# A two-block transformer kernel: its input in four pieces on ScalarE's queue, turned one chunk at a time

## The chip, the cores and the metric

The kernel runs on one core of one Trainium2 chip. The metric is the time of one execution on the device in microseconds, the median of several runs. The engines are PE (TensorE, matmul and transpose), DVE (VectorE), ACT (ScalarE), POOL (GpSimd) and SP (SyncE, which here only issues DMAs). ACT and POOL can issue DMAs too.

## The reference

There are 256 tokens of 1024 columns in float32. The first block is an RMS norm, one projection, two attentions in parallel (one with rotary keys per head, one with low-rank latents), gates, an output projection and an MLP. The second block is a gated mixer with a dilated attention, then a product-key expert layer over 16384 experts. What matters here is only how the first block begins:

```python
h = _rms_norm(x, g_pre_mix[l])          # x * rsqrt(mean(x*x) + eps) * g
proj = h @ w_in[l]                      # 1024 x 4256
qa, ka, va, c_q, c_kv, k_r, gate_logits = _split_cols(proj, ...)
```

The factor of each row, rsqrt(mean(x*x) + eps), is applied to the result of the projection, so that the multiplication can start before it is known. Only the gain g goes into the operand.

## The kernel before

**Data.** X is the input in SBUF, two tiles of 128 tokens by 1024 columns. For the projections it must stand with its columns on the partitions: PE transposes chunk c (128 columns of both tiles, two transposes, line 471) into a PSUM bank, ACT reads the bank, multiplies by the gain and writes the rounded high half TH (line 974), DVE computes the rest TL (line 1405). Every weight unit (128 rows of up to 1024 columns) is treated the same way: a DMA of SP brings it into one of four buffers `raw`, ACT rounds it into `whi` (line 968), DVE computes `wlo` (line 1396). `split(u)` in ACT's and DVE's programs is this step; each has three buffers. A product then is three matmuls: TH x whi, TH x wlo, TL x whi (line 453 where the weights move, `rows`).

**Order.** Every engine has a program written out by hand, and the programs meet by semaphores only. The first projection has eight units IN_A + k of 672 columns (336 KB each); unit k multiplies chunk k of X, 12 matmuls of 336 columns. Then come twelve units of 1024 columns (512 KB each), 12 matmuls of 512 columns. A counter s runs over the steps: one per unit for the first eight, two per unit afterwards. At each step every engine does its part of the main work and then `beside(s)`, which holds the work that goes on beside the projections: for PE, ACT and DVE those are the functions of that name. For the first eight steps ACT and DVE do `split(s + 2)`, then `beside(s)`.

**The start.** SP issues cst (identity and other constants, 148 KB), X columns 0 to 255, posi (the positions, 1 KB), unit 0, X columns 256 to 511, X columns 512 to 1023, and then the other units as their buffers come free. POOL issues ppc (the gains, 34.5 KB), mask_c (256 KB) and gb1 (a vector spread over 128 partitions, 512 KB). PE turns chunks 0 to 3 ahead of unit 0 and chunks 4 to 7 behind it (`beside(0)`). ACT loads its first function table at its first activation.

**The row factor.** ACT squares and sums tile 0 of X (line 977) at s = 2, behind `warm(ACT.Sqrt)`, which loads the table of the square root; DVE does tile 1 at s = 3. At s = 4 the factor r1 is worked out, at s = 5 two diagonal matrices of it, and at s = 7 PE multiplies them with ones (line 547) so that the factor stands along the free axis (rbc). At s = 8 to 10 DVE copies rbc and works out the angles of the rotation from posi. r1 is first needed when the results of the eight units are read (s = 8).

## Time and profile before

| | |
|---|---|
| median of 3 runs | 1370.74 us (1369.51 to 1370.87) |
| the profiled execution | 1368.58 us, its span 1366.8 us |
| PE busy | 1316.4 us, 96% of the span |
| DVE, ACT busy | 943.5 us (69%), 690.4 us (51%) |
| DMA | 260.55 MB, mean 191 GB/s |

The span runs from the first to the last instruction of the profiled execution, and all times in the trace count from its start. Busy time of an engine is the sum of its instructions. In a timeline a row is a run of equal instructions: start, time from the first start to the last end, engine, line, operation, result and operands, count, and in brackets how long the engine was idle before and what released it.

### The profile page before, as it was taken

Reading aid. Unit: us, or ns where it says so; the run is one execution under the profiler, and the core shown is the slowest. Engines: PE = TensorE matmul, PEld = TensorE weight load, DVE = VectorE, ACT = ScalarE, POOL = GpSimd, SP = SyncE. Lnnn points to the kernel's source line nnn. Section 1 sums busy time; section 2 is a strip of 40 time slices with the busy share of each in tenths; the row PEclk is TensorE's granted clock in tenths of the full one; section 3 lists DMA queues with packets and bytes.
Section 4 is the critical chain, followed back from the end, with each engine's and each line's share of the span. In section 5 each row is a group of like instructions: output and inputs, shape, how many; then the busy total and the mean of one; then the engine's idle time right before and its main releaser. Section 6 shows DMA issues by size and latency. Waiting matters only on the chain.

```text
span 1366.8 us, 22018 instructions
## 1 busy us (share of the span) xinstructions
PE 1316.4 (96%) x8592; PEld 1200.9 (88%) x8592; DVE 943.5 (69%) x1792; ACT 690.4 (51%) x1135; POOL 33.1 (2%) x27
## 2 busy tenths in 40 slices
PE   7999998999989899999999999999999999999996
PEld 6889978998877678999999999999988888888885
DVE  5765676674456755999899666676667676767665
ACT  5566456664455744444454444444444545454553
POOL 0000130000020000000000000000000000000000
PEclk9999999999999998999999999999999999999999
DMA  7533455666646335477767655555567676766763
GB/s 241 165 122 111 141 171 155 184 184 187 194 147 195 126 102 174 145 237 228 228 218 237 190 169 170 185 171 157 169 225 264 234 245 234 248 249 239 244 235 106
DMA packets 72662, 260.55 MB, mean 191 GB/s; under 512 B 8224, under 2 KB 8864, under 8 KB 72304
## 3 DMA queue, kind: packets, MB, share of 16 engines
q1 hardware_dynamic: 71520, 255.77, 57.7%
q0 software_dynamic: 1040, 3.38, 0.8%
q8 instruction: 69, 1.13, 0.3%
q14 instruction: 33, 0.27, 0.1%
HBM read 240.25 MB, written 18.87 MB: 190 GB/s over the span
## 4 chain that ended last, share of the span: by engine, by line
PE 87%; DVE 5%; ACT 4%; DMA 2%; issue 1%; SPq 0%; DVEq 0%; ACTq 0%
PE ps L933 24%; PE ps L453 14%; PE ps L461 13%; PE ps L462 13%; PE ps L463 13%; PE ps L916 4%; ACT whi L968 1%; PE ps L496 1%; DVE wlo L1396 1%; DVE mg L1654 1%; DMA raw<-in_expert_v_dram 1%; PE ps L471 1%; DMA raw<-in_w_in_dram 1%; PE ps L477 1%; DMA X<-in_x_dram 1%
## 5 line engine op out<-in xcount | busy, mean ns | idle before, releaser
L1396 DVE TENSOR_TENSOR wlo<-raw,whi 128x1024 fp32r<-128x1024 f32 (+2 forms) x410 | 498.0, 1216 | 352.8 <-ACT whi L968 350.7
L968 ACT ACTIVATE whi<-raw 128x1024 fp32r<-128x1024 f32 (+2 forms) x421 | 441.5, 1050 | 443.6 <-PE ps L463 166.0
L461 PE MATMUL ps<-TH,whi 128*128 128x256 f32 x1536 | 443.3, 289 | 2.3 <-DVE TL L1405 1.2
L462 PE MATMUL ps<-TL,whi 128*128 128x256 f32 x1536 | 436.3, 284 | 0.0
L463 PE MATMUL ps<-TH,wlo 128*128 128x256 f32 x1536 | 435.8, 284 | 0.0
L461 PEld LDWEIGHTS ps<-TH,whi 128*128 128x128 f32 x1536 | 296.9, 193 | 3.2 <-issue 3.0
L462 PEld LDWEIGHTS ps<-TL,whi 128*128 128x128 f32 x1536 | 296.3, 193 | 0.0
L463 PEld LDWEIGHTS ps<-TH,wlo 128*128 128x128 f32 x1536 | 295.7, 193 | 0.0
L933 PE MATMUL ps<-whi,TH 128*128 128x512 f32 x512 | 199.5, 390 | 5.2 <-DVE wlo L1396 3.7
L933 PE MATMUL ps<-whi,TL 128*128 128x512 f32 x512 | 199.2, 389 | 0.0
L933 PE MATMUL ps<-wlo,TH 128*128 128x512 f32 x512 | 199.2, 389 | 0.0
L933 PEld LDWEIGHTS ps<-whi,TH 128*128 128x128 f32 x512 | 96.1, 188 | 26.1 <-DVE wlo L1396 4.5
L933 PEld LDWEIGHTS ps<-whi,TL 128*128 128x128 f32 x512 | 96.1, 188 | 20.1
L933 PEld LDWEIGHTS ps<-wlo,TH 128*128 128x128 f32 x512 | 96.1, 188 | 19.7
L1334 ACT ACTIVATE ACTV<-ps 128x512 f32<-128x512 f32 x64 | 38.3, 598 | 123.9 <-PE ps L916 123.9
L453 PE MATMUL ps<-whi,TH 128*128 128x512 f32 (+1 forms) x208 | 79.1, 393 | 6.5 <-DVE wlo L1396 2.7
L453 PE MATMUL ps<-wlo,TH 128*128 128x512 f32 (+1 forms) x208 | 77.1, 383 | 0.0
L453 PE MATMUL ps<-whi,TL 128*128 128x512 f32 (+1 forms) x208 | 77.0, 383 | 0.0
L916 PE MATMUL ps<-X 128*128 128x128 f16 x512 | 70.7, 296 | 0.1
L2013 DVE TENSOR_TENSOR TL<-ACTV,TH 128x256 fp32r<-128x256 f32 x128 | 55.6, 434 | 0.5 <-ACT TH L974 0.5
L916 PEld LDWEIGHTS ps<-X 128*128 128x128 f16 x512 | 52.2, 118 | 3.6 <-DVE X L1999 0.3
L2009 DVE TENSOR_TENSOR ACTV<-ACTV,stage 128x256 f32<-128x256 f32 x128 | 53.6, 420 | 1.7 <-ACT ACTV L1334 1.7
(292 smaller groups left out, 1365.3 us busy)
## 6 DMA issues: line engine op xcount, KB each, us to landing
raw<-in_expert_u_dram SPq DMA_DIRECT2D x128, 512.0 KB, 3.7
raw<-in_expert_v_dram SPq DMA_DIRECT2D x128, 512.0 KB, 3.6
raw<-in_w_up_dram SPq DMA_DIRECT2D x32, 512.0 KB, 3.7
raw<-in_w_down_dram SPq DMA_DIRECT2D x32, 512.0 KB, 4.3
acts<-stage SPq DMA_DIRECT2D x32, 512.0 KB, 4.1
stage<-acts SPq DMA_DIRECT2D x30, 512.0 KB, 3.3
raw<-in_w_in_dram SPq DMA_DIRECT2D x20, 512.0 KB, 4.3
raw<-in_w_gate_dram SPq DMA_DIRECT2D x16, 512.0 KB, 3.5
```

Of the source, the lines that this page charges most:

```text
L453: m = e.matmul(o, x[:, k0 + j, sl], w[:, h, c:c + step], start=first, stop=last)
L461: e.matmul(dst, whi[:, h, sl], xh[:, k, :], start=k == 0, stop=False)
L462: e.matmul(dst, whi[:, h, sl], xl[:, k, :], start=False, stop=False)
L463: m = e.matmul(dst, wlo[:, h, sl], xh[:, k, :], start=False, stop=k == kn - 1)
L471: m = e.transpose(ps[b][:, at + t * 128:at + t * 128 + 128], src[:, t, c * 128:c * 128 + 128], ident)
L916: m = e.matmul(ps[g % 4][:, i * 128:i * 128 + 128], room[:, g % 2, 0, :, i], room[:, g % 2, w, :, i], start=w == 1, stop=w == 2)
L933: m = e.matmul(ps[bank4(t, d)][:, :], x[:, n % 8, sl], w[:, h, d * 512:d * 512 + 512], start=n == 0 and k == 0, stop=n == 127 and k == 2)
L968: e.activation(whi[:, u % NH, 0:n], raw[:, u % NR, 0:n], ACT.Copy).then_inc(*hi(u))
L1334: e.activation(ACTV[:, :, 4 * g:4 * g + 4], ps[g % 4][:, :].rearrange("p (t k) -> p k t", t=4), ACT.Copy, scale=1.0 / G_SCALE).then_inc(*w ...
L1396: e.tensor_tensor(wlo[:, u % NH, 0:n], raw[:, u % NR, 0:n], whi[:, u % NH, 0:n].bitcast(F32), ALU.subtract).then_inc(*lo(u))
L2009: e.tensor_tensor(ACTV[:, v, :], ACTV[:, v, :], stage[:, v % 8, :], ALU.mult).then_inc(*taken_v(i))
L2013: e.tensor_tensor(TL[:, i % 8, :], ACTV[:, V_ORDER[i], :], TH[:, i % 8, :].bitcast(F32), ALU.subtract).then_inc(*cut_d(i))
```

## The change

X comes in four pieces of 1, 1, 2 and 4 chunks, issued by ACT at its very start. SP issues only the identity ahead of the weight units, and the rest of cst behind unit 3. posi moves from SP to POOL, and POOL issues posi, mask_c and gb1 only when TL of chunk 5 is written. DVE writes a tile of zeros, and PE multiplies it four times (128 rows, 512 columns, into bank 7, whose content nothing reads) before it waits for the identity. ACT's first function table is loaded by `warm(ACT.Copy)` right behind its DMA issues. PE turns chunks 0 and 1 ahead of unit 0 and chunk s + 2 behind unit s; the banks are 4 to 7 in turn. In steps 0 to 5 ACT and DVE do `beside(s)`, now with chunk s + 2, ahead of `split(s + 2)`. The squares move to s = 5, r1 to s = 6, the diagonals to s = 7, rbc and the angles to s = 9.

```diff
--- before.py
+++ after.py
@@ -140,6 +140,9 @@
 
         ident = cs("ident")
         x_rows = A["x"].rearrange("(t p) d -> p t d", p=128)
+
+        X_PIECES = [(0, 1), (1, 2), (2, 4), (4, 8)]
+        PIECE_OF = [0, 1, 2, 2, 3, 3, 3, 3]
         warm_in, warm_out = stat(1), stat(1)
 
 
@@ -166,6 +169,7 @@
         PT1 = sb(p1, "PT", [128, 2, 8, 128])
         o1 = sb(p1, "o1", [128, 2, 512])
         gb1 = sb(p1, "gb1", [128, 1024])
+        zeros = sb(p1, "zeros", [128, 512], F32R)
         posi = sb(p1, "posi", [128, 2], I32)
         posf = sb(p1, "posf", [128, 2])
         ang = sb(p1, "ang", [128, 2, 24])
@@ -303,8 +307,8 @@
 
 
 
-        d_cst, d_ppc, d_pos, d_gb1, d_mask_c = (landing(n) for n in ("cst", "ppc", "pos", "gb1", "mask_c"))
-        d_x = [landing(f"x{i}") for i in range(3)]
+        d_ident, d_cst, d_ppc, d_pos, d_gb1, d_mask_c = (landing(n) for n in ("ident", "cst", "ppc", "pos", "gb1", "mask_c"))
+        d_x = [landing(f"x{i}") for i in range(4)]
         d_raw = [landing(f"raw{i}", range(i, UNITS, NR)) for i in range(NR)]
         d_gb2, d_gb4, d_cos, d_sin, d_mask_d, d_lng, d_lnb, d_ws, d_sub = (
             landing(n) for n in ("gb2", "gb4", "cos2", "sin2", "mask_d", "lng", "lnb", "ws", "sub"))
@@ -399,9 +403,9 @@
         out_d = signal("out_d", (
             "moba0r moba0 moba1r moba1 mla0r mla0 mla1r mla1 dil0r dil0 dil1r dil1").split())
         norm_d = signal("norm_d", (
-            "ones ss1 v1 r1 diag0 diag1 rbc pos ang0 ang1 turns whole less0 less1 less2 held folded angles "
-            "cq.ss cq.v cq.r cq ck.ss ck.v ck.r ck out.v out.r rsq down.v down.r ab.v ab.r x4.v x4.r x4.0 "
-            "x4.1").split())
+            "ones zeros ss1 v1 r1 diag0 diag1 rbc pos ang0 ang1 turns whole less0 less1 less2 held folded "
+            "angles cq.ss cq.v cq.r cq ck.ss ck.v ck.r ck out.v out.r rsq down.v down.r ab.v ab.r x4.v x4.r "
+            "x4.0 x4.1").split())
         rows_d = signal("rows_d", (
             "lat1 lat3 q k v uq0 uq1 uq2 ukv0 ukv1 q2 k2 v2.0 v2.1").split())
         gate_d = signal("gate_d", range(16))
@@ -499,11 +503,19 @@
 
 
 
-            e.wait_ge(*d_cst.at(0))
-            for c in range(4):
-                if c % 2 == 0:
-                    e.wait_ge(*d_x[c // 2].at(0))
-                turn(X, c, 4 + c).then_inc(*turned(f"x{c}"))
+            e.wait_ge(*norm_d.at("zeros"))
+            for _ in range(4):
+                e.matmul(ps[7][:, :], zeros[:, 0:128], zeros[:, :], start=True, stop=True)
+
+            def turn_x(c):
+                e.wait_ge(*d_x[PIECE_OF[c]].at(0))
+                if c >= 4:
+                    e.wait_ge(*low.at(f"x{c - 4}"))
+                turn(X, c, 4 + c % 4).then_inc(*turned(f"x{c}"))
+
+            e.wait_ge(*d_ident.at(0))
+            turn_x(0)
+            turn_x(1)
 
             def causal_attention(a, n):
 
@@ -537,12 +549,9 @@
 
             def beside(s):
 
-                if s == 0:
-                    e.wait_ge(*d_x[2].at(0))
-                    for c in range(4, 8):
-                        e.wait_ge(*low.at(f"x{c - 4}"))
-                        turn(X, c, c).then_inc(*turned(f"x{c}"))
-                elif s == 7:
+                if s < 6:
+                    turn_x(s + 2)
+                elif s == 9:
                     e.wait_ge(*norm_d.at("diag1"))
                     e.matmul(ps[7][:, 0:256], mg[:, 0, 0, 0:128], mg[:, 1, 0, :], start=True, stop=True).then_inc(*turned("rbc"))
                 elif s == 15:
@@ -998,13 +1007,21 @@
 
 
 
+            for i, (c0, c1) in enumerate(X_PIECES):
+                e.dma_start(X[:, :, c0 * 128:c1 * 128], x_rows[:, :, c0 * 128:c1 * 128]).then_inc(*d_x[i](0))
+            e.wait_ge(*norm_d.at("ones"))
+            warm(ACT.Copy)
+            gain_x = lambda c: pp("g_pre_mix", c)
+
+            def high_x(c):
+                e.wait_ge(*turned.at(f"x{c}"))
+                high_of("x", c, 4 + c % 4, 0, gain_x, TH)
+
             e.wait_ge(*d_ppc.at(0))
-            gain_x = lambda c: pp("g_pre_mix", c)
-            for c in range(4):
-                e.wait_ge(*turned.at(f"x{c}"))
-                high_of("x", c, 4 + c, 0, gain_x, TH)
-                if c % 2:
-                    split(c // 2)
+            high_x(0)
+            split(0)
+            high_x(1)
+            split(1)
 
             def causal_attention(a, n):
                 if n == 3:
@@ -1022,17 +1039,14 @@
                     probs(a, 1, 1, 5)
 
             def beside(s):
-                if s in (0, 1):
-                    for c in (4 + 2 * s, 5 + 2 * s):
-                        e.wait_ge(*turned.at(f"x{c}"))
-                        high_of("x", c, c, 0, gain_x, TH)
-                elif s == 2:
-                    e.wait_ge(*norm_d.at("ones"))
+                if s < 6:
+                    high_x(s + 2)
+                if s == 5:
                     warm(ACT.Sqrt)
-                    for i in range(3):
+                    for i in range(4):
                         e.wait_ge(*d_x[i].at(0))
                     square(SB1[:, 0:4, :].rearrange("p a b -> p (a b)"), X[:, 0, :], ss1[:, 0:1]).then_inc(*norm_a("ss1"))
-                elif s == 4:
+                elif s == 6:
                     e.wait_ge(*norm_d.at("v1"))
                     e.activation(s1, v1, ACT.Sqrt).then_inc(*norm_a("s1"))
                 elif s in (11, 19):
@@ -1120,6 +1134,10 @@
                     e.activation(sg[:, m, :], mg[:, m % 2, 0, :], ACT.Tanh, bias=hb[:, m:m + 1], scale=0.5).then_inc(*gate_a(m))
 
             for s in range(82):
+                if s < 6:
+                    beside(s)
+                    split(s + 2)
+                    continue
                 if s < 8:
                     split(s + 2)
                 elif s % 2 == 0:
@@ -1455,12 +1473,17 @@
 
 
             e.memset(warm_in, 1.0).then_inc(*norm_d("ones"))
+            e.memset(zeros[:, :].bitcast(F32), 0.0).then_inc(*norm_d("zeros"))
+            gain_x = lambda c: pp("g_pre_mix", c)
+
+            def low_x(c):
+                low_of("x", c, 4 + c % 4, 0, gain_x, TH, TL)
+
             e.wait_ge(*d_ppc.at(0))
-            gain_x = lambda c: pp("g_pre_mix", c)
-            for c in range(4):
-                low_of("x", c, 4 + c, 0, gain_x, TH, TL)
-                if c % 2:
-                    split(c // 2)
+            low_x(0)
+            split(0)
+            low_x(1)
+            split(1)
             e.tensor_scalar(hb[:, :], ppc[:, PPC["b_gate"][0]:PPC["b_gate"][1]], 0.5, None, ALU.mult)
 
             def causal_attention(a, n):
@@ -1479,26 +1502,25 @@
                     outs(a, 1, 6)
 
             def beside(s):
-                if s in (0, 1):
-                    for c in (4 + 2 * s, 5 + 2 * s):
-                        low_of("x", c, c, 0, gain_x, TH, TL)
-                elif s == 3:
-                    for i in range(3):
+                if s < 6:
+                    low_x(s + 2)
+                if s == 5:
+                    for i in range(4):
                         e.wait_ge(*d_x[i].at(0))
                     square_sum(SB1[:, 4:8, :].rearrange("p a b -> p (a b)"), X[:, 1, :], ss1[:, 1:2]).then_inc(*norm_d("ss1"))
-                elif s == 4:
+                elif s == 6:
                     e.wait_ge(*norm_a.at("ss1"))
                     e.wait_ge(*norm_d.at("ss1"))
                     mean_eps(v1, ss1, 1024).then_inc(*norm_d("v1"))
                     e.wait_ge(*norm_a.at("s1"))
                     e.reciprocal(r1, s1).then_inc(*norm_d("r1"))
-                elif s == 5:
+                elif s == 7:
                     e.memset(mg[:, 0, 0, 0:128], 1.0)
                     e.wait_ge(*norm_d.at("r1"))
                     e.wait_ge(*d_cst.at(0))
                     for t in range(2):
                         scaled_copy(mg[:, 1, 0, t * 128:t * 128 + 128], ident, r1[:, t:t + 1]).then_inc(*norm_d(f"diag{t}"))
-                elif s == 8:
+                elif s == 9:
                     e.wait_ge(*turned.at("rbc"))
                     e.tensor_copy(rbc[:, :], ps[7][:, 0:256]).then_inc(*norm_d("rbc"))
                     e.wait_ge(*d_pos.at(0))
@@ -1510,7 +1532,6 @@
                     e.tensor_scalar(an2[:, :, :], ang[:, :, :], INV2PI, MAGIC, ALU.mult, ALU.add).then_inc(*norm_d("turns"))
                     e.wait_ge(*norm_d.at("turns"))
                     e.tensor_scalar(an3[:, :, :], an2[:, :, :], MAGIC, None, ALU.subtract).then_inc(*norm_d("whole"))
-                elif s == 9:
                     for i, c in enumerate((PI_A, PI_B, PI_C)):
                         e.wait_ge(*norm_d.at(f"less{i - 1}" if i else "whole"))
                         e.scalar_tensor_tensor(out=ang[:, :, :], in0=an3[:, :, :], scalar=-c, in1=ang[:, :, :],
@@ -1628,6 +1649,10 @@
                                        op0=ALU.add, op1=ALU.mult).then_inc(*scaled_d(n))
 
             for s in range(82):
+                if s < 6:
+                    beside(s)
+                    split(s + 2)
+                    continue
                 if s < 8:
                     split(s + 2)
                 elif s % 2 == 0:
@@ -2078,6 +2103,8 @@
                                 ALU.subtract).then_inc(*lo_pool(u))
 
             e.dma_start(ppc[:, :], A["ppc"]).then_inc(*d_ppc(0))
+            e.wait_ge(*low.at("x5"))
+            e.dma_start(posi[:, :], A["positions"]).then_inc(*d_pos(0))
             e.dma_start(mask_c[:, :, :], A["causal"]).then_inc(*d_mask_c(0))
             e.dma_start(gb1[:, :], A["g_post_mix"].partition_broadcast(128)).then_inc(*d_gb1(0))
             for u in (BR_B + 1, BR_B + 2, BR_B + 3, OUT, OUT + 1, UP, UP + 1):
@@ -2114,9 +2141,6 @@
                         e.wait_ge(*lo.at(u - NR))
                 e.dma_start(raw[:, u % NR, 0:width(u)], units[u]).then_inc(*d_raw[u % NR](u))
 
-            def load_x(i, c0, c1):
-                e.dma_start(X[:, :, c0:c1], x_rows[:, :, c0:c1]).then_inc(*d_x[i](0))
-
             def store(j):
                 e.wait_ge(*gelu_u.at(4 * j + 3))
                 e.dma_start(acts[j], stage[:, 4 * (j % 2):4 * (j % 2) + 4, :]).then_inc(*d_store[j % 2](j))
@@ -2128,14 +2152,11 @@
                 e.wait_ge(*taken_v.at(4 * j + 3))
                 e.dma_start(stage[:, 4 * (j % 2):4 * (j % 2) + 4, :], acts[j]).then_inc(*d_fetch[j % 2](j))
 
-            e.dma_start(cst[:, :], A["cst"]).then_inc(*d_cst(0))
-            load_x(0, 0, 256)
-            e.dma_start(posi[:, :], A["positions"]).then_inc(*d_pos(0))
-            load(0)
-            load_x(1, 256, 512)
-            load_x(2, 512, 1024)
-            for u in range(1, QUERY + 4):
+            e.dma_start(ident, A["cst"][:, 0:128]).then_inc(*d_ident(0))
+            for u in range(QUERY + 4):
                 load(u)
+                if u == 3:
+                    e.dma_start(cst[:, 128:CST_W], A["cst"][:, 128:CST_W]).then_inc(*d_cst(0))
             e.wait_ge(*norm_a.at("x4.1"))
             e.wait_ge(*norm_d.at("x4.1"))
             e.wait_ge(*last_d.at("11"))
```

## Rows read from the trace of the kernel before

**Rows 1.** The page: the chain of work that ended last, by line.
```profile
PE ps L933 24%; PE ps L453 14%; PE ps L461 13%; PE ps L462 13%; PE ps L463 13%; PE ps L916 4%; ACT whi L968 1%; PE ps L496 1%; DVE wlo L1396 1%; DVE mg L1654 1%; DMA raw<-in_expert_v_dram 1%; PE ps L471 1%; DMA raw<-in_w_in_dram 1%; PE ps L477 1%; DMA X<-in_x_dram 1%
```

**Rows 2.** Windows of the start: length, busy us of each engine, PEclk, DMA share, GB/s.
```profile
8.00:10.00 2.00, 0.00 (x0) 0.00 (x0) 0.86 (x1) 0.76 (x1) 0.00 (x0) 1.00 1.03 366
...
20.00:24.00 4.00, 4.00 (x28) 4.00 (x27) 2.27 (x4) 2.35 (x4) 0.00 (x0) 1.00 0.63 151
```

**Rows 3.** Timeline of the start, 0 to 24 us.
```profile
1.26 0.68 POOL L2080 DMA_DIRECT2D ppc<-in_ppc_dram  x1 [0.81 <-POOLq L2262]
1.66 0.46 SPq L2133 DMA_DIRECT2D posi<-in_positions_dram  x1
...
4.04 1.09 PE L471 MATMUL ps<-cst,X 128*128 128x128 f32 x4 [4.04 <-DMA X<-in_x_dram]
4.79 1.28 ACT L974 ACT_TABLE_LOAD   x1 [4.79 <-PE ps L471]
6.08 0.84 ACT L974 ACTIVATE TH<-ps,ppc 128x256 fp32r<-128x256 f32 x2
...
8.23 0.76 ACT L968 ACTIVATE whi<-raw 128x672 fp32r<-128x672 f32 x1 [1.31 <-DMA raw<-in_w_in_a_dram]
9.02 0.86 DVE L1396 TENSOR_TENSOR wlo<-raw,whi 128x672 fp32r<-128x672 f32 x1 [1.48 <-ACT whi L968]
...
10.05 1.12 PE L471 MATMUL ps<-cst,X 128*128 128x128 f32 x4 [4.92 <-DMA X<-in_x_dram]
...
10.82 0.91 PE L453 MATMUL ps<-whi,TH 128*128 128x336 f32 x2
...
14.32 1.45 PE L471 MATMUL ps<-cst,X 128*128 128x128 f32 x8
...
15.53 0.56 PE L453 MATMUL ps<-whi,TH 128*128 128x336 f32 x2
...
18.50 1.28 ACT L971 ACT_TABLE_LOAD   x1
...
20.95 1.41 ACT L968 ACTIVATE whi<-raw 128x672 fp32r<-128x672 f32 x2
```

**Rows 4.** Waits of PE over the whole span: total us, times, longest.
```profile
PE ps L471 <- DMA X<-in_x_dram: 9.0, 2, 4.9
PE ps L471 <- DVE X L1686: 6.4, 2, 3.4
...
PE ps L471 <- ACT xn L974: 3.2, 1, 3.2
```

**Rows 5.** Timeline of PE, 24 to 48 us.
```profile
28.50 0.59 PE L547 MATMUL ps<-mg 128*128 128x256 f32 x2
28.74 0.58 PE L453 MATMUL ps<-whi,TH 128*128 128x512 f32 x1
...
39.84 0.60 PE L471 MATMUL ps<-cst,pj 128*128 128x128 f32 x4
40.20 0.48 PE L453 MATMUL ps<-whi,TH 128*128 128x512 f32 x1
...
43.53 0.44 PE L471 MATMUL ps<-cst,pj 128*128 128x128 f32 x2 [0.34 <-DVE CQl L1405]
```

**Rows 6.** Windows behind three pauses of PE: length, PE busy, PEclk, DMA.
```profile
209.80:216.50 6.70, 5.36 (x24) 0.50 0.23 76
...
400.90:404.20 3.30, 3.30 (x13) 0.50 0.02 5
...
513.60:523.70 10.10, 7.87 (x36) 0.50 0.68 208
```

**Rows 7.** DMA issues of the first 2.2 us: count, KB, us to landing.
```profile
raw<-in_w_in_a_dram SPq DMA_DIRECT2D x1, 336.0 KB, 6.0
X<-in_x_dram SPq DMA_DIRECT2D x1, 256.0 KB, 2.7
...
ppc<-in_ppc_dram POOLq DMA_DIRECT2D x1, 34.5 KB, 2.8
```

## The prediction

> **What bounds the kernel now.** I read the page's chain first: almost all of it is PE's dense work, and of the start there is only "PE ps L471" and "DMA X", 1% each [rows 1]. A change at the start can be worth no more than what it takes out of the first microseconds, and it keeps that only if PE, once it runs, is not made to wait again. So I read the start by stretches [rows 2], then the timeline to 24 us [rows 3], then who waits for whom [rows 4], the timeline to 44 us, where the old and the new order of work meet again [rows 5], and what PE's clock did after earlier pauses [rows 6].
>
> From 8 to 10 us PE has nothing while the DMA engines are over 100% busy [rows 2]. The waiter is L471, the transposes of X: twice, at most 4.9 us [rows 4]. From 10.05 on PE works without a gap. The first projection starts at 10.82, the last of the eight input units ends at 28.50, the two matmuls of L547 follow, and the next twelve units start at 28.74 [rows 3, 5]. PE is slow at first: rows 0 take 3.50 us (10.82 to 14.32), while the seven units from 15.53 to 28.50 take 1.85 each. So the engine ran at 1.2 GHz and then at 2.4 (the profile's own clock reads 1.00 throughout and is no help here). When did it rise? The eight transposes at 14.32 take 1.21 us to the next row; at the low level they would take 1.54 (four in 0.77, 10.05 to 10.82), at the high one 0.72 (four in 0.36, 39.84 to 40.20 in [rows 5]). So it rose at about 15.2, 5.1 us after PE began to work unbroken.
>
> **Part 1, the start.** ACT now issues four DMAs before anything else. SP's issues take about 0.46, POOL's first 0.68 [rows 3]. ACT's queue is a plain one like SP's, so I take 0.46: 0.75 to 2.6 us. The table load, 1.28, moves there too, from 4.79, where it was on the path; with 0.2 for the warm-up ACT is free at 4.1 (at POOL's price 5.0). The first x piece is half of the 256 KB that landed 2.7 us after their issue [rows 7]; issued at 0.75 it lands at 3.0 to 3.5 and is turned 0.75 later (4.04 to 4.79). ppc is issued as before, at 1.26, and lands 2.8 later, at 4.1. So the first high part runs 4.15 to 4.6. The first weight unit leaves SP right behind the identity, at 1.2. Before, it left at 2.16, behind posi, and took 6.0 us [rows 7], beside mask_c and the broadcast of gb1, which are both held back now. Bounds for its landing: 2.7 us, as X's piece, gives 3.9; 6.0 gives 7.2. Beside it now stands up to 1 MB of x on its own queue, in place of 0.77 MB of constants; but it starts 1 us earlier into emptier engines. I take 3.5 us, 4.7. Then whi 0.76, wlo 0.86 and hand-overs: the first projection starts at **6.4** against 10.82, **4.4 us earlier** (6.1 to 8.9 by the bounds).
>
> The Trainium skill, "DMA: Bandwidth & Descriptors", section "Issuing engines are not separate DMA queues", says that DMAs of several issuers run on the same 16 engines and interleave, so that a second issuer saves only issue time. The full engines of [rows 2] agree. By that rule alone part 1 would gain from what is held back and from SP's issue time, nothing else.
>
> POOL now waits for low x5 (about 18 us) ahead of posi, mask_c and gb1; behind them on POOL stand only its own splits, the first that of unit 46. posi is first read by DVE after rows 7, mask_c and gb1 far later. The 0.77 MB takes 2.1 us at the 366 GB/s of [rows 2], at a time when the engines are 63% busy and a weight unit has over 4 us between issue and split. The rest of cst lands long before the diagonals behind step 7. All this: nothing. The memset of 512 columns of zeros takes less than the 0.86 of a 672-column DVE pass, and DVE has nothing to do until 4.6. Four matmuls of 512 columns at the low clock take 4 x 0.44 by the 3.50/12 of a 336-column one: 1.8 us, over by 3.5, in PE's wait for x. Nothing as long as x lands no earlier; at most 0.5.
>
> **Part 2, chunk by chunk.** PE turns chunk k+2 behind rows k, ACT then does high x(k+2) and splits unit k+2, DVE the low halves. From the end of rows k: two transposes 0.44 ([rows 5], at 43.53), high 0.42, whi 0.76, wlo 0.86, hand-overs 0.09. Rows k+2 may start **2.57** after the end of rows k. PE has rows k+1 (1.84 at 2.4 GHz) and one or two turns of 0.18 until then, so about every second unit waits 0.37. With the clock up 5.1 us after 6.4, at 11.5: rows 0 run 6.4 to 9.9, a turn 0.39, rows 1 to 12.71 (1.2 us at the low level, 34% of it, the rest fast), rows 2 12.89 to 14.73, rows 3 15.28 to 17.12, rows 4 17.30 to 19.14, rows 5 19.69 to 21.53, rows 6 21.71 to 23.55.
>
> **Part 3, the square.** At step 5 ACT does high x7, then warm(Sqrt), the square of X, and only then split(7). Before, the same block stood behind split(4) and delayed only split(5): 18.50 to 20.95, with wlo 5 ready at 22.6 (20.95 + 0.76 + 0.86) for rows 5 at 22.9, just hidden. Now what queues behind it is the very unit that PE wants next but one. From the end of rows 5: transposes 0.44, high 0.47, table load, warm and square 2.45, whi 0.76, wlo 0.86, hand-overs 0.09. Rows 7 start **5.07** later, at 26.60. PE has only rows 6, until 23.55: it **stands 3.05 us**. DVE's own square lies inside ACT's block. Rows 7 end at 28.44, against 28.50: **-0.06**. In terms: -4.42 start; +0.74 two waits of 0.37; +3.05; +0.57 rows 1 still partly slow; +0.08 turns; the rest is rounding.
>
> **Part 4, behind it.** The rbc matmul moves from behind unit 7 to behind unit 8, 0.24 either way. wlo 8 is done about 6.5 after the end of rows 5, and rows 8 start at 6.91. On DVE the reciprocal, the diagonals, the rbc copy, the angles and the cq norm come later relative to PE. Bounds 0 and 0.5; PE idled 0.34 at 43.53 for CQl anyway, which takes up a small delay. I take nothing.
>
> **Part 5, the clock.** A standing PE has a second price. Three times PE stood that long: 6.4 us in two pauses of which the longer was 3.4, and one of 3.2 [rows 4]; each time the granted clock was then 0.50, that is 1.2 GHz, for stretches of 6.7, 3.3 and 10.1 us [rows 6]. Part 3 makes a fourth such pause. The shortest stretch costs half its length, **1.7**, since dense rows 7 and 8 follow. Bounds: 0 (no fall; here the pause lies between dense rows, there short transposes with further pauses followed) and 5. I take 1.7, by three falls out of three.
>
> Sum: -0.06 + 1.7 = +1.6. The profiled execution took 1368.58 (its span 1366.8 and 1.8 around it), 2.2 below the median of 1370.74; on it the sum makes 1370.2. On the median, which I forecast, it makes **1372.4**.
>
> **The rivals.**
> *No fall.* The pause comes, the clock stays: -0.06, 1370.7. For it: dense matmuls on both sides.
> *The zeros lift the clock early.* PE then has matmuls or turns from 1.7 to about 5 us. If it runs at 2.4 GHz from 6.4 on, the chain of 2.57 sets the pace: rows 0 end at 8.24, rows 1 run 8.5 to 10.34, rows 2 10.81 to 12.65, rows 3 end at 14.75, rows 4 at 17.06, rows 5 at 19.16, rows 7 at 26.07: -2.4, 1368.3, or 1370.0 with a fall. Against it: PE stands from 5 to 6.4, and the 1.09 us of transposes at 4.04 lifted nothing. The Trainium skill, "TensorE: Matmul & The Clock Gate", Part 1, says that the low level is the default and that activity lifts it, and Part 4 that transposes do not count as such; the rise after the dense stretch from 10.05 goes with the first. By it this rival hangs on the zeros alone.
> *The slow side: x beside the weights.* x's four pieces take a share of every DMA engine, so the first weight unit again lands 6.0 us after its issue, at 7.2. Rows 0 start at 8.9, +2.5: 1374.9 with the fall, 1373.2 without. For it: the engines are full before PE starts. Against it: fewer bytes ahead. With the fall it decides (over +0.2%) from a landing at 5.8.
> *Much faster.* The clock is up early, does not fall, and the pause is shorter than 3.05 or the start earlier than 6.4: under 1368.
>
> **How the numbers follow.** A measurement of this kernel can tell about 0.2% (2.7 us) from no change. Forecast 0.38, no fall 0.26, early clock 0.16, x beside the weights 0.13, much faster 0.07. The range 1368.1 to 1374.2 holds the first three with most of their bounds and leaves out most of the last two. Faster (below 1368.0): 0.07 and 0.04 of the early clock. Slower (above 1373.5): 0.09 of x beside the weights and 0.07 of the forecast with a longer low stretch. So 0.11, 0.73, 0.16.
>
> **What the new profile would show.** The table load before 4; x0 turned near 4.1; the first L453 near 6.4; two idles of PE of some 0.4; then one of 3 us near 24, released by DVE wlo behind ACT whi behind the square; PEclk 0.50 right after it; rows 7 ending within 1 us of 28.5. I am wrong if the first weight unit lands after 5.8, if the clock is up before 8, or if the pause is under 2 us.

## The result, and the profile after

The changed kernel took **1371.34 us** (median of 20 runs, 1366.99 to 1375.79). The kernel before, run beside it on the same chips, took 1368.15 (20 runs, 1363.71 to 1370.87). The ratio is **1.0027**, with an interval of 1.0015 to 1.0039: some 3.7 us slower (the two medians stand 3.2 apart). The forecast was 1372.4, that is 1.7 above the median shown with it, 1370.74; the direction and the mechanism held, and the size was about half. That the 1372.4 itself lies within 1.1 us of the measured median is in part luck: the kernel before came out 2.6 us lower this time. The profiled execution has a span of 1369.8 us against 1366.8.

**The start** (timeline of the changed kernel; it answers to [rows 3]; L475 is the transpose, L457 the projection, L983 the high half, L977 and L1414 the two halves of a weight unit):

```profile
0.74 2.03 ACTq L1011 DMA_DIRECT2D X<-in_x_dram  x4
...
1.25 0.68 POOL L2105 DMA_DIRECT2D ppc<-in_ppc_dram  x1 [0.80 <-POOLq L2283]
...
1.49 2.07 PE L508 MATMUL ps<-zeros 128*128 128x512 f32 x4 [1.49 <-DVE zeros L1476]
2.79 1.28 ACT L980 ACT_TABLE_LOAD   x1 [2.79 <-issue]
...
3.90 0.66 PE L475 MATMUL ps<-cst,X 128*128 128x128 f32 x2 [0.34 <-DMA X<-in_x_dram]
...
5.03 0.69 PE L475 MATMUL ps<-cst,X 128*128 128x128 f32 x2 [0.47 <-DMA X<-in_x_dram]
6.11 0.47 ACT L983 ACTIVATE TH<-ps,ppc 128x256 fp32r<-128x256 f32 x1 [1.82 <-DMA ppc<-in_ppc_dram]
6.48 0.75 ACT L977 ACTIVATE whi<-raw 128x672 fp32r<-128x672 f32 x1
...
8.18 0.93 PE L457 MATMUL ps<-whi,TH 128*128 128x336 f32 x2 [2.46 <-DVE wlo L1414]
...
13.81 0.72 PE L457 MATMUL ps<-whi,TH 128*128 128x336 f32 x2
...
14.37 0.47 PE L457 MATMUL ps<-wlo,TH 128*128 128x336 f32 x2
```

The issues, the table load and x0 come as forecast. Then ACT stands for 1.82 us, and what it waits for is ppc, the smallest transfer of the start. The DMA issues of the first 3 us (count, KB, us from issue to landing; beside [rows 7]):

```profile
raw<-in_w_in_a_dram SPq DMA_DIRECT2D x4, 336.0 KB, 6.2
X<-in_x_dram ACTq DMA_DIRECT2D x1, 512.0 KB, 8.7
X<-in_x_dram ACTq DMA_DIRECT2D x2, 128.0 KB, 3.4
...
ppc<-in_ppc_dram POOLq DMA_DIRECT2D x1, 34.5 KB, 4.8
```

ppc took 4.8 us here and 2.8 before. The first projection starts at 8.18, which is 2.6 us earlier than before [rows 3] and not 4.4. The step in the durations, 0.72 to 0.47, shows that PE's clock rose at about 14.4.

**The pause** (same timeline). The two short waits for the chain, which stand at the weight loads of rows 3 and rows 5, and the long one:

```profile
17.48 0.30 PEld L457 LDWEIGHTS ps<-whi,TH 128*128 128x128 f32 x2 [0.29 <-DVE wlo L1414]
...
21.93 0.30 PEld L457 LDWEIGHTS ps<-whi,TH 128*128 128x128 f32 x2 [0.29 <-DVE wlo L1414]
...
24.79 1.28 ACT L980 ACT_TABLE_LOAD   x1
...
26.19 1.04 ACT L986 ACTIVATE SB<-X 128x1024 f32<-128x1024 f32 x1
...
27.23 1.69 ACT L977 ACTIVATE whi<-raw 128x672 fp32r<-128x672 f32 x2
28.01 2.17 DVE L1414 TENSOR_TENSOR wlo<-raw,whi 128x672 fp32r<-128x672 f32 x2 [1.58 <-ACT whi L977]
...
28.92 0.93 PE L457 MATMUL ps<-whi,TH 128*128 128x336 f32 x2 [2.82 <-DVE wlo L1414]
```

In this order it reads as one chain: table load, square, whi 7, wlo 7, and PE's rows 7 at 28.92, after 2.82 us in which PE has nothing. In the windows around it (length, PE busy, PEclk, DMA share, GB/s) the granted clock falls within the pause and is back at 34.9. The 0.85 of the second window is 0.8 us at the low clock, so that the low stretch runs from 28.0 to 34.85, 6.8 us:

```profile
23.00:26.00 3.00, 3.00 (x21) 1.00 0.92 314
26.20:28.80 2.60, 0.00 (x0) 0.85 0.79 303
28.90:34.80 5.90, 5.88 (x18) 0.50 0.72 215
34.90:38.00 3.10, 3.10 (x15) 1.00 0.71 234
```

From 28.92 to 34.85 PE is 100% busy at 1.2 GHz. That is 5.93 us for 2.97 us of work at 2.4 GHz.

**The meeting point.** From the first cq transposes on, both kernels do the same in the same order. They stood at 39.84 [rows 5]:

```profile
44.97 0.60 PE L475 MATMUL ps<-cst,pj 128*128 128x128 f32 x4
48.66 0.44 PE L475 MATMUL ps<-cst,pj 128*128 128x128 f32 x2 [0.34 <-DVE CQl L1423]
```

So the changed kernel is 5.1 us late there. It keeps this offset until about 200 us, where the stretches of low clock begin that the kernel before has too [rows 6]. Those of the changed kernel, in windows as above:

```profile
215.80:222.50 6.70, 5.57 (x26) 0.50 0.24 81
403.50:410.20 6.70, 5.69 (x22) 0.50 0.17 69
519.50:522.90 3.40, 2.82 (x14) 0.51 0.48 193
```

Together they are 16.8 us against 20.1 in [rows 6]. The offset at the end is 3.0 us, not 5.1; half the difference of the stretches is 1.7 of these 2.1. Between the stretches the starts of PE's instructions run parallel in the two traces, but for two steps of 0.5 us, near 424 and 1020 us.

### The profile page after: what moved, and what is told of

It is laid out like the page before. It is cut to its first block, busy times and chain, and to the rows that moved or that the text cites. A ratio compares the mean times of both kernels' runs of the same rounds, so it can differ in the third digit from the quotient of the medians.

```text
span 1369.8 us, 22035 instructions
## 1 busy us (share of the span) xinstructions
PE 1322.0 (97%) x8596; PEld 1203.8 (88%) x8596; DVE 944.5 (69%) x1793; ACT 690.5 (50%) x1136; POOL 33.6 (2%) x28
## 3 DMA queue, kind: packets, MB, share of 16 engines
q10 hardware_dynamic: 1088, 1.05, 0.2%
## 4 chain that ended last, share of the span: by engine, by line
PE 86%; DVE 6%; ACT 5%; DMA 2%; issue 2%; DVEq 0%; SPq 0%; ACTq 0%; POOLq 0%
PE ps L942 24%; PE ps L457 14%; PE ps L465 13%; PE ps L466 13%; PE ps L467 13%; PE ps L925 4%; ACT whi L977 1%; DVE wlo L1414 1%; PE ps L500 1%; DVE mg L1679 1%; PE ps L481 1%; PE ps L878 1%; DMA raw<-in_w_in_dram 1%; PE ps L493 0%; DMA raw<-in_expert_v_dram 0%
## 5 line engine op out<-in xcount | busy, mean ns | idle before, releaser
L1414 DVE TENSOR_TENSOR wlo<-raw,whi 128x1024 fp32r<-128x1024 f32 (+2 forms) x410 | 497.9, 1216 | 348.6 <-ACT whi L977 346.3
L977 ACT ACTIVATE whi<-raw 128x1024 fp32r<-128x1024 f32 (+2 forms) x421 | 441.7, 1051 | 440.4 <-PE ps L467 164.7
L942 PEld LDWEIGHTS ps<-whi,TH 128*128 128x128 f32 x512 | 96.1, 188 | 25.7 <-DVE wlo L1414 3.9
L457 PE MATMUL ps<-whi,TH 128*128 128x512 f32 (+1 forms) x208 | 81.5, 405 | 11.3 <-DVE wlo L1414 7.5
L457 PE MATMUL ps<-wlo,TH 128*128 128x512 f32 (+1 forms) x208 | 78.5, 391 | 0.0
L457 PE MATMUL ps<-whi,TL 128*128 128x512 f32 (+1 forms) x208 | 78.2, 390 | 0.0
L457 PEld LDWEIGHTS ps<-whi,TH 128*128 128x128 f32 x208 | 40.4, 199 | 21.2 <-DVE wlo L1414 9.6
```

The lines of the kernel that those rows point to most:

```text
L457: m = e.matmul(o, x[:, k0 + j, sl], w[:, h, c:c + step], start=first, stop=last)
L942: m = e.matmul(ps[bank4(t, d)][:, :], x[:, n % 8, sl], w[:, h, d * 512:d * 512 + 512], start=n == 0 and k == 0, stop=n == 127 and k == 2)
L977: e.activation(whi[:, u % NH, 0:n], raw[:, u % NR, 0:n], ACT.Copy).then_inc(*hi(u))
L1414: e.tensor_tensor(wlo[:, u % NH, 0:n], raw[:, u % NR, 0:n], whi[:, u % NH, 0:n].bitcast(F32), ALU.subtract).then_inc(*lo(u))
```

## The experiments

Each is one edit to the changed kernel, except the last two, which edit the kernel before. In the table, "start" is the first projection, "pause" PE's idle time at rows 7, "low" what the granted clock spent at 1.2 GHz right behind it, "cq" the meeting point in the profiled execution, and the ratio is the timed one against the kernel before, with its interval. All but the ratio come from one execution each.

| | start | pause | low | cq | ratio |
|---|---|---|---|---|---|
| before | 10.82 | none | none | 39.84 | 1 |
| after | 8.18 | 2.82 | 6.8 | 44.97 | 1.0027 (1.0015 to 1.0039) |
| square_late | 8.69 | 0.28 | none | 40.64 | 1.0007 (0.9993 to 1.0022) |
| fill_pause | 7.28 | filled | none | 39.96 | 1.0010 (0.9995 to 1.0026) |
| sqrt_first | 7.68 | 1.31 | none | 39.87 | 1.0008 (0.9995 to 1.0021) |
| ppc_sp | 8.88 | 2.81 | none | 42.78 | 1.0035 (1.0017 to 1.0053) |
| no_zeros | 7.90 | 2.83 | 6.8 | 44.64 | 1.0026 (1.0010 to 1.0042) |
| bridge | 8.11 | 2.52 | 3.4 | 41.15 | 1.0037 (1.0024 to 1.0050) |
| staged | 7.13 | 2.82 | 3.4 | 42.53 | 1.0014 (0.9998 to 1.0031) |
| early_const | 8.14 | 2.52 | 3.4 | 42.79 | 1.0023 (1.0007 to 1.0038) |
| all_moved | 7.32 | 0.27 | none | 39.07 | 1.0013 (0.9999 to 1.0027) |
| all_moved_bridge | 7.28 | 0.20 | none | 38.52 | 0.9996 (0.9984 to 1.0009) |
| before_zeros | 11.20 | none | none | 39.12 | 0.9989 (0.9973 to 1.0006) |
| before_fill | 10.75 | none | none | 38.81 | 0.9986 (0.9968 to 1.0003) |

Single executions differ where no edit makes them differ. In the seven in which x, unit 0 and ppc are issued as in the changed kernel (after, square_late, fill_pause, sqrt_first, no_zeros, early_const, bridge), ppc took 3.9 to 5.3 us and the start fell between 7.28 and 8.69. In the eight with just the four matmuls by zero (after, square_late, fill_pause, sqrt_first, ppc_sp, staged, early_const, all_moved) the clock rose 3.1 to 6.2 us after the start. A difference between two executions that is smaller than this shows little by itself.

### The square behind the weights: square_late

```diff
-                if s == 5:                    # ACT; DVE's square_sum alike
+                elif s == 7:
                     warm(ACT.Sqrt)
...
                     square(SB1[:, 0:4, :].rearrange("p a b -> p (a b)"), X[:, 0, :], ss1[:, 0:1])
```

The factor r1 and the diagonals follow in the same step, behind the split of unit 9.

> The changed kernel with one thing moved: ACT's square block (warm Sqrt, square, root) and DVE's part of it go from steps 5 and 6 to step 7, behind split(9), with the diagonals behind them. Theory A, the pause behind the square and the fall of the clock after it are the loss: no idle of PE above 0.6 us between rows 0 and rows 11, no granted clock of 0.50 before 60 us; the first L-transpose of cq, at 44.97 in the changed kernel, comes at 39.0 to 39.7 (2.8 of pause and 3.0 of low clock gone), and the kernel is about 5 us faster than the changed one, 0.9985 of before. Rival B, the loss is in the later rbc, angles and norm or in the held-back transfers: those are untouched or later still, cq stays above 43 and the time within 1 us of the changed kernel, 1.002 to 1.003 of before.

The pause is gone, and so is the low stretch:

```profile
26.86 0.58 PE L457 MATMUL ps<-whi,TH 128*128 128x336 f32 x2 [0.28 <-DVE wlo L1413]
40.64 0.66 PE L475 MATMUL ps<-cst,pj 128*128 128x128 f32 x4
45.04 0.44 PE L475 MATMUL ps<-cst,pj 128*128 128x128 f32 x2 [1.00 <-DVE CQl L1422]
```

Although this execution started 0.5 us later than the changed kernel's, it is 4.3 us earlier at the meeting point. So in the trace the place of the square makes the loss. The cq norm now comes later: the wait for CQl grew from 0.34 to 1.00, so that behind it the offset to the kernel before is 1.5 us, not 0.8 (45.04 against 43.53 in [rows 5]). The meeting point is above what was expected in part because the start was 0.5 later, and the time is that of the kernel before, no better; 0.9985 was expected. The timed interval overlaps that of the changed kernel. But the three edits that take away the pause, half of it or the fall behind it (this one and the next two) have ratios of 1.0007 to 1.0010, and the kernels that keep the pause 1.0014 to 1.0037.

### The pause filled: fill_pause

```diff
+                elif s == 6:                  # PE, behind rows 6
+                    for _ in range(12):
+                        e.matmul(ps[4][:, :], zeros[:, 0:128], zeros[:, :], start=True, stop=True)
```

> The changed kernel with 12 more matmuls of zeros (128x512, into a free bank) behind rows 6, so that PE works through the pause: 12 x 0.23 = 2.7 us of work in a wait of 2.8. It prices the clock alone. Theory A, the fall is a price of its own on top of the pause: no 0.50 stretch, rows 7 start within 0.2 us of the changed kernel's time after the end of rows 6, and cq comes 2.5 to 3.4 us earlier than 44.97, at 41.6 to 42.5; 1.0005 of before. Rival C, the low stretch only covers time that would be waited anyway (ACT and DVE set the pace there): cq moves under 1 us, ratio as the changed kernel's, 1.003.

ACT and DVE are as late as in the changed kernel; only PE does not stand idle meanwhile:

```profile
23.93 2.93 PE L556 MATMUL ps<-zeros 128*128 128x512 f32 x12
```

No low stretch followed. From start to meeting point are 32.7 us, against 36.8 in the changed kernel. Of these 4.1 us 1.3 are there when rows 7 start (19.4 us after the start against 20.7; the clock rose 3.1 us behind the start, not 6.2), and 2.8 come behind that, where the low stretch is missing. This separates the two prices of one pause: the standing itself stays (rows 7 start 5.15 us after the end of rows 5, against 5.04), the clock is the other. That no fall came could be chance in one execution, as ppc_sp below shows. The timed ratio is 0.17% below the changed kernel's, but the two intervals overlap.

### The table loaded once: sqrt_first

```diff
-            warm(ACT.Copy)
+            warm(ACT.Sqrt)                    # at ACT's start; none at step 5
```

> The changed kernel with ACT's first warm-up on Sqrt in place of Copy, and the warm-up of Sqrt at step 5 left out: one table load fewer, and the block between high x7 and split(7) shorter by 1.4 us (1.28 load and 0.11). Theory A: the pause of 2.8 us shrinks to 1.4; whether the clock still falls is open, cq at 43.6 if it does, 40.6 if not. If the first rounding after the square root's table needs a load of its own, it shows at 4 us as a second load of 1.28 and the start moves little, since ACT waits for ppc until 6.1. Rival B: cq within 0.5 us of 44.97.

Only one table load is in the trace, at 2.78, and the copies and the square ran behind it. The pause shrank by 1.51, the 1.28 of the load and the 0.2 of the warm-up, and behind a pause of 1.31 us the clock did not fall:

```profile
26.53 0.57 PE L457 MATMUL ps<-whi,TH 128*128 128x336 f32 x2 [1.31 <-DVE wlo L1413]
```

### ppc ahead of the weights: ppc_sp

```diff
             e.dma_start(ident, A["cst"][:, 0:128]).then_inc(*d_ident(0))
+            e.dma_start(ppc[:, :], A["ppc"]).then_inc(*d_ppc(0))      # SP; taken away from POOL
```

> The changed kernel with ppc (the gains) issued by SP right behind the identity, not by POOL. In the changed kernel ACT stood from 4.29 to 6.11 for ppc, which took 4.8 us to land. Theory D, ppc is what made the start 1.8 us later than forecast: ppc lands by 4.2, the first projection starts at 6.6 to 6.9 in place of 8.18, everything to the pause comes 1.3 to 1.6 earlier, the pause stays 2.8; 1 to 1.5 us faster than the changed kernel. Rival E, the weights' landing sets the start anyway: the first unit, now 0.5 later out of SP, lands at 5.2 or later and the projection starts at 7.2 to 8.2, gain under 1 us.

ppc landed at 3.6 and no longer held ACT. The row of unit 0, issued at 1.66 now, and that of ppc:

```profile
raw<-in_w_in_a_dram SPq DMA_DIRECT2D x1, 336.0 KB, 5.5
...
ppc<-in_ppc_dram SPq DMA_DIRECT2D x1, 34.5 KB, 2.4
```

Unit 0 took 5.5 us, where that of the changed kernel, issued at 1.19, took 3.4. ACT stood 2.37 us for it, and the start came at 8.88, later than with ppc late. In the seven executions with ppc on POOL unit 0 took 3.1 to 3.5 us, so its 5.5 lie outside their scatter. Getting one transfer out of the way put another in its place. Why 34.5 KB ahead of it cost unit 0 some 2 us was not found. The Trainium skill, "DMA: Bandwidth & Descriptors", section "Issuing engines are not separate DMA queues", says that DMAs of all issuers interleave on the same 16 engines; that the engines are 91 to 99% busy in the changed kernel from 2 to 8 us agrees with it.

The second finding is what did not happen. Behind a pause of 2.81 us the clock stayed up:

```profile
26.60:29.30 2.70, 0.02 (x1) 1.00 0.87 323
29.40:35.00 5.60, 5.57 (x28) 1.00 0.73 204
```

### The zeros taken out: no_zeros

```diff
-            e.wait_ge(*norm_d.at("zeros"))
-            for _ in range(4):
-                e.matmul(ps[7][:, :], zeros[:, 0:128], zeros[:, :], start=True, stop=True)
```

> The changed kernel without the four matmuls of zeros (the memset stays). Theory F, they do nothing as they stand, since PE waits from 5.7 to 8.2 us behind them: the clock rises 3 to 6.2 us after the first projection, the range of the five profiles so far, x0 is turned up to 0.5 us earlier because PE is free at 3.1, the start does not move since ACT waits for ppc, and the time is within 1 us of the changed kernel's. Rival: they lift the clock earlier in part of the executions: without them the time is 1 to 2 us longer.

The clock rose at about 14.1, 6.2 us behind the start, as in the changed kernel, and the timed ratio is the changed kernel's. So the four matmuls by zero did nothing that shows. How much they move the rise one execution can't say, since with them it came 3.1 to 6.2 us after the start.

### More zeros: bridge

```diff
             turn_x(1)
+            for _ in range(6):
+                e.matmul(ps[7][:, :], zeros[:, 0:128], zeros[:, :], start=True, stop=True)
```

> The changed kernel with six more matmuls of zeros behind the turn of chunk 1 (6 x 0.43 = 2.6 us at the low clock), so that PE works from 1.5 us to the first projection almost without a gap. Theory F, it is the gap from 5.7 to 8.2 us that keeps the four zero matmuls from lifting the clock: the pair of 128x336 matmuls takes 0.47 in place of 0.76 from 9 us at the latest (14.4 in the changed kernel), rows 0 and 1 then take 1.85 to 2.6 and 1.85, and rows 2 start 1.5 to 2.5 us earlier relative to rows 0. The pause of 2.8 stays and grows no shorter; the time is 1 to 2.5 us below the changed kernel's. Rival G, zeros do not lift the clock (its rise hangs on something else): the rise comes 5 to 6 us after the first projection as before and the time is the changed kernel's within 1 us.

Now the first pairs of projections show the step, 0.9 us after the start:

```profile
8.11 0.93 PE L457 MATMUL ps<-whi,TH 128*128 128x336 f32 x2
8.83 0.54 PE L457 MATMUL ps<-wlo,TH 128*128 128x336 f32 x2
9.21 0.47 PE L457 MATMUL ps<-whi,TL 128*128 128x336 f32 x2
```

The 0.9 us lie outside the 3.1 to 6.2 of the eight executions above, and before_zeros below shows the same. So zeros do lift the clock where little stands between them and the work. The Trainium skill, "TensorE: Matmul & The Clock Gate", Part 1, says that activity lifts it from its low default, and this agrees. At the meeting point this execution is 3.8 us ahead of the changed kernel's, and in time its ratio is the highest of all, beside ppc_sp's. Its stretches of low clock behind 200 us:

```profile
210.40:220.50 10.10, 8.66 (x40) 0.50 0.26 75
401.50:404.90 3.40, 3.35 (x16) 0.50 0.13 52
480.00:483.40 3.40, 3.40 (x10) 0.50 0.62 200
517.60:527.70 10.10, 8.18 (x37) 0.50 0.69 227
1353.80:1357.10 3.30, 3.27 (x8) 0.51 0.49 155
```

They are 30.3 us, against 16.8 in the changed kernel and 20.1 in the kernel before: what the start gained is given back there. (Half of the 10.2 on top of the 1.3 at the meeting point would be 6.4; the span is 4.9 longer than before, since PE is not busy through all of them.) This is no accident of one execution: its ten runs lie close together (1371.69 to 1373.50), and the granted clock averaged over a run is 0.986 to 0.989 in all ten, against 0.986 to 0.994 (median 0.9905) in the twenty of the changed kernel. Why these stretches became longer was not found.

### x behind the first weights: staged

```diff
-            for i, (c0, c1) in enumerate(X_PIECES):          # ACT
+            for i, (c0, c1) in enumerate(X_PIECES[:2]):
...
+            load(0)                                          # SP
+            e.wait_ge(*d_ppc.at(0))
+            for u in range(1, QUERY + 4):                    # x2 behind unit 1, x3 behind unit 2
```

> The changed kernel with the transfers of the start staged: ACT issues only the first two x pieces; SP issues the identity and unit 0, then waits for ppc, and then unit 1, x chunks 2 and 3, unit 2, x chunks 4 to 7, unit 3. Theory H, what stands beside them makes ppc (4.8 us in the changed kernel) and unit 0 (up to 7.15 when ppc went first on SP) land late: now ppc lands by 4.3, unit 0 by 4.7, the first projection starts at 6.3 to 6.9 in place of 7.3 to 8.9 over the five profiles. Unit 1 lands by 8, before rows 1 at about 10. Time 1 to 1.5 us below the changed kernel's, the pause of 2.8 stays. Rival I, POOL's queue is slow by itself: ppc lands at 5.2 or later even with few transfers beside it.

With fewer bytes under way unit 0 took 3.3 us, as with all of x, and ppc still 3.8. ppc landed at 5.0 instead of 6.1, and the start came earlier by just that much, at 7.13; 4.3 and 6.3 to 6.9 were expected. This is the earliest start of all, but fill_pause, with all of x under way, had 7.28 and 3.9 us for ppc. With all_moved and all_moved_bridge (7.32, 7.28) three executions with x staged lie at the early end, which speaks for an effect without showing its size. Unit 3 then landed late (PE stood 0.47 at rows 3), and the pause behind the square is unchanged, as it must be. The low stretch was the shorter one this time:

```profile
28.40:31.70 3.30, 3.30 (x12) 0.50 0.75 214
31.80:36.00 4.20, 4.20 (x20) 1.00 0.79 251
```

### The constants not held back: early_const

```diff
             e.dma_start(ppc[:, :], A["ppc"]).then_inc(*d_ppc(0))
-            e.wait_ge(*low.at("x5"))
             e.dma_start(posi[:, :], A["positions"]).then_inc(*d_pos(0))
```

> The changed kernel with posi, mask_c and gb1 not held back (POOL issues them right behind ppc, as before). Theory H, the constants in the start lengthen it: 0.77 MB more ahead of unit 1 and the later x pieces, unit 0 lands at 5 to 7 in place of 4.6, x chunks 4 to 7 above 12, the first projection 0 to 2 us later than 8.18; the pause stays. Time 0 to 2 us above the changed kernel's. Rival B, that held-back transfers collide with the weights at 21 to 27 us and cost there: the time falls by 1 us or more.

The start is at 8.14 (changed kernel 8.18). The 512 KB piece of x took 11.3 us, not 8.7, but no engine needs it so early. Holding back 0.77 MB brought nothing that shows.

### Everything moved: all_moved and all_moved_bridge

The first is staged, with the square late, the table loaded once, and ppc on SP behind unit 0. The second has three more matmuls by zero behind the turn of chunk 1.

> All that the experiments so far point to, in one kernel: the staged transfers, ppc on SP behind unit 0, the warm-up on Sqrt at the start, the square block in step 7. Theory A: each part brings what it brought alone. ppc lands at 4 to 4.5, unit 0 at 4.6, the first projection starts at 6.5 to 6.9; no idle above 0.6 us up to the transposes of cq, no fall of the clock before 60 us; these come at 37.5 to 38.8 (39.84 before). The time is 1 to 2 us below before: ratio 0.998 to 1.000. Rival J, the gain of the start is given back even so, since turning chunk by chunk ties each split to the unit two ahead (2.57 us after each unit) and the clock rises later relative to the work: cq at 39.5 or later, ratio 1.000 to 1.001.

> The same with three more matmuls of zeros (1.3 us) behind the turn of chunk 1, which ends at about 5.6. Theory F: PE works from 1.5 us on almost without a gap, the clock is up by 9 us as in the run with six such matmuls (there 9.0), rows 0 and 1 are fast for the most part, cq at 36.5 to 38; ratio 0.997 to 0.999. If the last matmuls of zeros hold rows 0 up, it is by under 0.3 us. Rival G, the early rise in that run was the luck of one execution: the clock is up 3 to 6 us after the first projection and cq as in the kernel without them.

Both reach the meeting point ahead of the kernel before, but only by 0.8 and 1.3 us, though they start 3.5 us earlier. The chain of 2.5 us for each two units takes most of the rest, and behind the meeting point the waits for CQl (1.00 and 0.98 instead of 0.34) take another 0.6, so that 0.1 and 0.6 are left (43.47 and 42.92 against 43.53). Neither timed ratio can be told from 1. The early rise that was expected of the three further matmuls (by 9 us) did not come: the clock rose at 11.1, 3.8 us after the start, within the range of the executions without them.

### The kernel before, with zeros: before_zeros and before_fill

```diff
+            e.wait_ge(*norm_d.at("zeros"))
+            multiply_zeros(4)
...
             for c in range(4):
+                if c == 2:
+                    multiply_zeros(12)
                 if c % 2 == 0:
                     e.wait_ge(*d_x[c // 2].at(0))
```

before_fill also puts 12 matmuls of TH by TH, of which nothing is read, ahead of the transposes of two later norms.

> The kernel before with nothing of the change but the zeros, and more of them: the memset, four matmuls before the wait for cst, and twelve more (4 to 5 us) between the transposes of chunk 1 and the wait for chunk 2, where PE stood 4.9 us. Theory F, dense zeros lift the clock and the rise is worth half of the low time behind 10.82: the clock is up by 10.5 us (15.2 before), rows 0 take 1.9 us in place of 3.5 and the transposes behind them 0.8 in place of 1.2; cq comes 1.5 to 2.4 us earlier than 39.84; ratio 0.998 to 0.9995. Rival G: the zeros do not matter, cq within 0.5 us of 39.84 and ratio 1.000; or the twelfth ends after 10.05 and the start is late by up to 0.3.

> The same, and twelve matmuls of whatever stands in TH (128x512, 2.7 us, into bank 4, which nothing reads then) in each of two of the three later pauses of PE, ahead of the transposes of h2 (3.05 us of idle, then 6.8 us of low clock in the profile of before) and of h3 (3.38, then 3.4). Their results are never read. Theory A, every long pause of PE is paid twice: no low stretch at 205 to 220 and 395 to 410, each worth 1.7 to 5.1 us; together with the start 4 to 7 us below before, ratio 0.995 to 0.9975. Rival C: the low stretches cover work that is not PE's, or the clock falls anyway in the transposes that follow: low stretches stay and the ratio is that of the kernel with zeros at the start alone.

In before_zeros the zeros run from 5.14 to 10.44, and rows 0 then take 1.93 us where they took 3.50. Of these 1.6 only 0.7 reached the meeting point, since x had landed later and rows 1 stood 0.61 for wlo. In the profiled execution of before_fill the pause at 204 is filled, and a low stretch came all the same, behind the short transposes that follow:

```profile
204.16 2.88 PE L718 MATMUL ps<-TH 128*128 128x512 f32 x12
207.39 1.07 PE L472 MATMUL ps<-cst,X 128*128 128x128 f32 x8 [0.35 <-DVE X L1703]
209.02 1.61 PE L472 MATMUL ps<-cst,X 128*128 128x128 f32 x8 [0.56 <-DVE TL L1421]
211.81 0.55 PE L462 MATMUL ps<-TH,whi 128*128 128x256 f32 x1 [1.18 <-issue]
```

The window behind it:

```profile
211.90:215.10 3.20, 3.20 (x15) 0.50 0.46 163
```

It lasted 3.4 us, as in before_zeros, where the kernel before had 6.8. Behind the second filled pause none came, where the kernel before has one [rows 6]:

```profile
400.90:404.20 3.30, 3.30 (x17) 1.00 0.04 10
```

But two of 3.4 us, at 423 and 478 us, are new. These two kernels have the lowest medians (1366.51 and 1365.51 against 1368.59 beside them), but both intervals include 1.

The trace hides something here, since it shows one of the slower executions. The mean granted clock of before_fill's twelve runs falls into two groups: 0.990 to 0.992 in five, which took 1366.60 to 1370.37 us (the profiled one among them), and 0.995 to 0.996 in seven, which took 1362.85 to 1365.64. No run of before_zeros is above 0.993, and of the 109 of the kernel before one reaches 0.995. So filling two pauses did take out low stretches in seven runs of twelve, and these came out at 0.996 to 0.998 of the kernel before, about what was expected. Which stretches they were is not known, as no such run was traced.

## Why the prediction was right, and where its sizes were off

**The start** was mis-sized. The step "ppc is issued as before, at 1.26, and lands 2.8 later, at 4.1" took its price from one execution of the old order, in which the DMA engines were 75% busy while ppc was under way, against 86% in the changed kernel: ppc landed 4.8 later, at 6.1. Three executions of the old order now give 2.8, 3.3 and 3.6 us, seven of the new one 3.9 to 5.3. The step that looked uncertain, the landing of unit 0 at 4.7, held. So the start came 1.8 us later than forecast. ppc_sp shows that this is not ppc's place alone: moved ahead, it sends unit 0 back to 7.15. That is the landing which the rival "x beside the weights" gave, but the rival itself did not come in the changed kernel, where unit 0 landed at 4.6; what was late was the one transfer whose price the prediction gave no bound. How much of this the bytes of x make, staged does not settle.

**Chunk by chunk** held: rows k + 2 start 2.49 and 2.50 us after the end of rows k (2.57 forecast), with two waits of 0.29 (0.37). The clock rose 6.2 us after the start, not 5.1, so that rows 1 took 3.0 us and not 2.4.

**The square** held nearly to the hundredth: rows 7 start 5.04 us after the end of rows 5, at 23.88 (5.07 forecast), and PE stands 2.82 (3.05). The difference is PE's side: from the end of rows 5, rows 6 with the turn took PE 2.2 us and not 2.0. square_late and sqrt_first show the cause by taking it away in two ways.

**The clock** was right in kind and mis-sized. "The shortest stretch costs half its length, 1.7": the stretch was the middle one and cost 3.0. In the other executions with a pause of 2.5 to 2.8 it was 6.8 once more, 3.4 three times, and once it did not come, so the 1.7 was a fair value and the "no fall" a real case; which of them comes in one execution is chance. That the pause brings the fall rests on counts: it came in five of the six executions with the long pause, and in none of the five in which the pause was short or filled.

**The sum at rows 7.** Forecast -0.06. Measured at full clock rows 7 would have ended at 28.92 + 1.84 = 30.76, against 28.50: +2.3. Of this 1.8 is the start and 0.6 the rise, less 0.16 for the shorter waits. With 3.0 for the fall it makes 5.3; the meeting point shows 5.1. Then 2.1 come back in the later stretches, which the prediction did not treat at all. It left 3.0 in the profile and 3.7 in the timed ratio, where 1.6 was forecast. So the sum for the start was short by 3.5 us at the meeting point, and that the whole came within 2.1 of it is owed to stretches that it left out. Of the signs named beforehand the early table load, the two short waits, the pause behind the square and the low clock after it came; the pause stood at 26.1 to 28.9 and not near 24, and rows 7 ended at 32.45, 4 us behind the 28.5 that they were to meet within 1. The rivals "the zeros lift the clock early" and "much faster" fell: PE stood from 5.7 to 8.2, and the clock rose 6.2 us after the start, which is no earlier than without zeros.

**What the change is worth without its flaw.** The start gain is real, but it doesn't reach the meeting point even without the pause: square_late starts 2.1 us before the kernel before and stands 0.8 behind it there. From the first projection to the end of the eighth unit it takes 20.12 us (8.69 to 28.81) instead of 17.68 (10.82 to 28.50). Three waits of 0.29 for the chain are 0.9 of this, and rows 1, in good part at the low clock (2.98 instead of 1.93), are 1.05; the kernel before has its transposes at that place. Most of the rest, 0.6, is in rows 2 to 7, which take 1.92 to 1.95 each behind a turn and 1.84 where nothing stands between them. Another 0.5 up to the meeting point lies in many small steps, and the later cq norm costs 0.7 more behind it. all_moved_bridge, with all mended, is 1.3 ahead at the meeting point and 0.6 once past the wait for CQl, too little to be told in 1368.

## What to carry to other kernels

An earlier start is worth what it still is at the point where old and new order meet: read that point first, and look for work on ACT or DVE (a table load, a reduction) that now stands ahead of the very operand PE wants next. A pause of PE has two prices, the pause and the slow stretch behind it. In a start in which several loads are under way together, look at what a load that is moved ahead does to the next one: here it sent the next one back by more than it gained. One trace can be the odd one among the runs; the granted clock of every run tells whether it is.

## What the runs showed of the hardware

- A pause of 2.5 to 2.8 us between dense matmuls was followed by low clock in five of six profiled executions, for 3.4 us (three times) or 6.8 (twice). Pauses of 0.2 to 1.3 us at this place brought none in the four executions that had them. The fall came within the pause in three, and 0.7 and 1.2 us after PE had gone on in the other two (staged and early_const).
- With four matmuls by zero followed by standing the clock rose 3.1 to 6.2 us after the first projection (eight executions), without them 6.2 (one). With six more, up to the first projection, it rose 0.9 us after, with three more 3.8. With sixteen in the kernel before it was up ahead of the first projection (two executions); without them it rose 4.3 us after it (one).
- A transfer of 34.5 KB took 2.8 to 3.6 us from issue to landing in the order of the kernel before (three executions), 3.9 to 5.3 in that of the changed kernel (seven), 3.5 to 3.8 with less of x under way (three), and 2.4 issued by SP ahead of the first weights.
- The copies of ACT needed no table of their own behind a load for the square root; one load of 1.28 us was saved.
- PE's instructions keep their spacing between the kernels from one low stretch to the next, but for a few steps of under 1 us. The time of a run goes with its mean granted clock: in the 109 runs of the kernel before beside the experiments the median is 1364.0 us at 0.994 (16 runs), 1368.1 at 0.991 (20) and 1372.0 at 0.987 (4). So most of the scatter from 1363 to 1374 us is time at the low clock.
- Open: what decides the number and length of the later stretches, and so why bridge, ahead at 41 us, is slowest at the end.
